# A hybrid layer's compression stage: the sample unit of its mixer spread over two steps, and ScalarE's work around a batch's change in another order

## What is computed

```python
def compress_rows(rows, pe, w1, w2):
    ch = rows[:, :n_chunks * CMP_STRIDE].reshape(B, n_chunks, CMP_STRIDE, G, D)
    proj = jnp.einsum('bnsgd,psdh->pbngh', ch, w1)
    bias = jnp.einsum('psd,psdh->ph', pe, w1)
    h = proj[0, :, 0:n_blk] + bias[0]
    for p in range(1, CMP_PARTS):
        h = h + proj[p, :, p:p + n_blk] + bias[p]
    return jnp.einsum('bngh,hd->bngd', jax.nn.silu(h), w2)
```

```python
def step(s, xs):
    qb, fb, kb, vb = xs
    a = jnp.cumsum(fb.astype(jnp.float32), axis=2)
    decay = jnp.exp(jnp.where(causal, a[:, :, :, None, :] - a[:, :, None, :, :], -jnp.inf))
    att = jnp.einsum('bhtk,bhsk,bhtsk->bhts', qb, kb, decay)
    o = jnp.einsum('bhts,bhsv->bhtv', att, vb) + jnp.einsum('bhtk,bhkv->bhtv', qb * jnp.exp(a), s)
    a_end = a[:, :, -1:, :]
    s = jnp.exp(a_end[:, :, 0, :, None]) * s + jnp.einsum('bhsk,bhsv->bhkv', kb * jnp.exp(a_end - a), vb)
    return s, o
```

## Time and profile before

| | |
|---|---|
| median of 3 runs | 2224.09 us (2223.43 to 2231.28) |
| the profiled execution, device time | 2235.45 us |
| its span, first to last instruction | 2233.7 us |
| TensorE (PE) busy | 2070.1 us, 93% of the span |
| VectorE (DVE) busy | 1455.1 us, 65% |
| ScalarE (ACT) busy | 1088.7 us, 49% |
| GpSimd (POOL) busy | 724.2 us, 32% |
| granted TensorE clock, mean | 0.959 |

### The profile page before, as it was taken

One profiled execution on the slowest core, in us unless ns is written; L12 is line 12 of the kernel. 1 busy time (PEld: TensorE's weight loads), 2 busy tenths in 40 slices (PEclk: granted clock), 3 DMA queues, 4 the chain that ended last, 5 costly groups with the idle time before them and its releaser, 6 DMA issues. The chain is left out here.

```text
span 2233.7 us, 43938 instructions
## 1 busy us (share of the span) xinstructions
PE 2070.1 (93%) x17158; PEld 1931.3 (86%) x17158; DVE 1455.1 (65%) x3124; ACT 1088.7 (49%) x2256; POOL 724.2 (32%) x996
## 2 busy tenths in 40 slices
PE   6999998999999999975889898997999999999997
PEld 5999997988888888864768786877999999999997
DVE  4222234876776776786588687458788788765667
ACT  4114223776776776744377476325333333334334
POOL 0001003766655665520089496120111111110000
PEclk9999998999999999987889799998999999999999
DMA  4115554766656656578310011331332332365342
GB/s 128 57 57 169 195 217 122 215 196 176 188 171 194 192 162 183 157 194 306 103 55 8 5 48 55 107 102 41 101 114 75 101 116 73 101 237 192 117 168 96
DMA packets 226053, 295.71 MB, mean 132 GB/s; under 512 B 23986, under 2 KB 161426, under 8 KB 224658
## 3 DMA queue, kind: packets, MB, share of 16 engines
q1 hardware_dynamic: 199224, 191.65, 28.1%
q0 software_dynamic: 26624, 101.27, 13.9%
HBM read 217.12 MB, written 82.63 MB: 134 GB/s over the span
## 5 line engine op out<-in xcount | busy, mean ns | idle before, releaser
L1568 POOL TENSOR_TENSOR C<-C,a_mt 128x264 f32<-128x264 f32 x66 | 69.2, 1069 | 407.6 <-ACT C L1653 271.9
L3520 PE MATMUL cplain<-a_XH,w1H 128*128 128x256 f32 x512 | 155.7, 304 | 6.4 <-ACT a_hs L3132 6.4
L2087 PE MATMUL f<-a_slot,wd_slot 128*128 128x264 f32 x1176 | 148.2, 285 | 1.6 <-DVE a_slot L1897 0.9
L2050 PE MATMUL f<-a_b,ring 128*128 128x264 f32 x1056 | 143.8, 286 | 4.3 <-DVE a_b L1793 3.7
L2087 PEld LDWEIGHTS f<-a_slot,wd_slot 128*128 128x128 f32 x1176 | 144.8, 188 | 2.5 <-issue 1.6
L3520 PE MATMUL cplain<-a_XL,w1H 128*128 128x256 f32 x512 | 144.9, 283 | 0.0
L3520 PE MATMUL cplain<-a_XH,w1L 128*128 128x256 f32 x512 | 144.6, 283 | 0.0
L3461 PE MATMUL cpt<-ident,X 128*128 128x128 f32 x768 | 119.8, 279 | 22.2 <-DVE a_KTL L3341 8.6
L2050 PEld LDWEIGHTS f<-a_b,ring 128*128 128x128 f32 x1056 | 135.3, 190 | 4.8 <-issue 4.8
L2917 POOL DMA_INDIRECT X<-in_cache_nsa_kv,idx x122 | 129.3, 1060 | 31.3 <-issue 24.2
L502 PE MATMUL pj<-wH,xL 128*128 128x256 f32 (+2 forms) x464 | 130.9, 282 | 0.0
(11 more groups left out here) (623 smaller groups left out, 6551.2 us busy)
## 6 DMA issues: line engine op xcount, KB each, us to landing
v_s<-X SPq DMA_DIRECT2D x64, 256.0 KB, 4.3
a_slot<-a_T SPq DMA_DIRECT2D x20, 792.0 KB, 4.6
raw<-in_w_in POOLq DMA_DIRECT2D x12, 1024.0 KB, 6.1
V<-v_s SPq DMA_DIRECT2D x6, 2048.0 KB, 12.1
raw<-in_w_gate SPq DMA_DIRECT2D x22, 512.0 KB, 5.2
raw_odd<-in_w_val SPq DMA_DIRECT2D x22, 512.0 KB, 6.1
a_T<-C SPq DMA_DIRECT2D x20, 528.0 KB, 3.5
a_T<-sums SPq DMA_DIRECT2D x11, 792.0 KB, 4.5
```

The lines of the kernel that those rows point to most:

```text
L1568: nc.gpsimd.tensor_tensor(C[j][:, at], C[j][:, at], mt[:, q % 2, m, c], ALU.mult).then_inc(multiplied, 1)
L2050: last = nc.tensor.matmul(out_bank(q, r, c), w[:, k], x[:, k], start=begins and k + part == 0, stop=k == 3 and part == 2, skip_group_check ...
L2087: last = nc.tensor.matmul(acc(u, o, h), x(n)[:, k, P * o:P * o + P], a(n)[:, k, HW * h:HW * h + HW], start=u in (0, 2, 4, 6) and begins an ...
L3520: last = nc.tensor.matmul(out[:, h], w, x, start=(begins and q + h + part == 0), stop=(ends and q + h == 2 and part == 2), skip_group_chec ...
```

## The change

Nothing that is computed changes; work changes its place.

- ScalarE: a new piece `load_silu` (one column of Silu into the new tile `tiny`) stands at the end of s=7, so that Silu's table is loaded there. `hidden(u - 1, 0)` moves from the end of s=1 to the end of s=0. The exponentials of the units move from the end of the steps s=3, 5, 7 to the end of s=2, 4, 6; those at s=1 stay. `keys_high` stands ahead of `high_sum`.
- VectorE: `keys` ahead of `low_sum`. For a sample unit, `results` in the odd step behind the first lower part, the first four updates at that step's end as before, and the last four in the next even step, ahead of its weighing.
- TensorE: for a sample unit `decode_products` stand ahead of the second half of `project_second` in the even step; `outputs` behind `project_first` of the odd step; the first half of the new states ahead of the second half of `project_second` there; their second half behind `project_first` of the next even step.

```diff
--- before.py
+++ after.py
@@ -2773,6 +2773,7 @@
         S0 = sb("S0", [P, DB, P])
         ob = sb("ob", [P, 3, P])
         osq = sb("osq", [P, P])
+        tiny = sb("tiny", [P, 1])
         rowsel = sb("rowsel", [DT, DB])
         tokb = sb("tokb", [P, DB, DT])
         normw = sb("normw", [P, HGW])
@@ -2810,7 +2811,7 @@
             "sub_ready", "exp_ready", "w_ready", "a_done", "post_step", "a_kept"))
         b_done, o_kept, s_ready2, sq_ready, sc_step, o_ready, vs_ready = (sem(n) for n in (
             "b_done", "o_kept", "s_ready2", "sq_ready", "sc_step", "o_ready", "vs_ready"))
-        d_done, d_kept = sem("d_done"), sem("d_kept")
+        d_done, d_kept, tiny_ready = sem("d_done"), sem("d_kept"), sem("tiny_ready")
 
         block = ctx.enter_context(nc.Block())
         cache = io["cache_nsa_kv"][0].rearrange("n (c t) s g d -> (n c) (t s g d)", t=2)
@@ -3132,6 +3133,12 @@
                     last = nc.scalar.activation(x, x if k == 0 else plain[m][:], ACT.Silu, bias=bias[:, 2 * k + m:2 * k + m + 1])
                 last.then_inc(hs_ready[k], 1)
 
+            def load_silu(u):
+                act.wait_ge(bias_kept, 1)
+                if u >= 1:
+                    act.wait_ge(tiny_ready, u)
+                nc.scalar.activation(tiny[:], bias[:, 0:1], ACT.Silu).then_inc(tiny_ready, 1)
+
             def hidden_prompt(k):
                 act.wait_ge(rows_turned, k + 1)
                 for m in range(2):
@@ -3218,14 +3225,16 @@
                     copy_turned(at + 1, 1)
                 split_high(at + 1, 1)
                 if at + 1 < PAIRS:
+                    keys_high(at + 1)
                     high_sum(at + 1)
-                    keys_high(at + 1)
-                if u >= 1 and s == 1:
-                    hidden(u - 1, 0)
-                if at % 2 == 1 and at // 2 + 1 < NN:
+                if (s == 1 or s % 2 == 0 and s > 0) and at // 2 + 1 < NN:
                     exponentials(at // 2 + 1)
                 if at % 2 == 0 and at >= 2:
                     squares(at // 2 - 1)
+                if u >= 1 and s == 0:
+                    hidden(u - 1, 0)
+                if s == NS - 1 and u < DB:
+                    load_silu(u)
             for k in range(2):
                 prompt_hidden_rows(k)
             squares(NN - 1)
@@ -3404,13 +3413,17 @@
                 if at + 1 < LAST:
                     upper_copy(at + 1, 0)
                 if at % 2 == 0:
-                    if n >= 1 and not decode(n - 1):
+                    if n >= 1 and decode(n - 1):
+                        decoded(n - 1, 1)
+                    elif n >= 1:
                         results(n - 1)
                     weigh(n)
                 elif not decode(n):
                     pairs(n)
                 if at + 1 < LAST:
                     low_part(at + 1, 0)
+                if at % 2 == 1 and decode(n):
+                    results(n)
                 if u >= 1 and s == 4:
                     keep_blocks(u - 1)
                 if s == NS - 1 and u < DB:
@@ -3419,8 +3432,8 @@
                     upper_copy(at + 1, 1)
                     low_part(at + 1, 1)
                 if at + 1 < PAIRS:
+                    keys(at + 1)
                     low_sum(at + 1)
-                    keys(at + 1)
                 if 1 <= u < DB - 1 and s == 1:
                     queries(u + 1)
                 if at % 2 == 0 and decode(n):
@@ -3429,14 +3442,14 @@
                         block_maxima(0, slice(16, 32))
                         for i in range(2):
                             block_maxima(1, slice(16 * i, 16 * i + 16))
-                    results(n)
                 elif decode(n):
-                    for half in range(2):
-                        if at == LAST - 1:
-                            block_maxima(half, slice(32, 48))
-                        decoded(n, half)
+                    if at == LAST - 1:
+                        for G in range(2):
+                            block_maxima(G, slice(32, 48))
+                    decoded(n, 0)
                 if at == LAST - 3:
                     block_maxima(0, slice(0, 16))
+            decoded(NN - 1, 1)
             for G in range(2):
                 block_maxima(G, slice(48, 64))
             keep_blocks(DB)
@@ -3661,6 +3674,10 @@
                 n = at // 2
                 turn(at + 1, 0)
                 project_first(at)
+                if at % 2 == 1 and decode(n):
+                    outputs(n)
+                elif at % 2 == 0 and n >= 1 and decode(n - 1):
+                    new_states(n - 1, 1)
                 if u >= 1 and s == 4:
                     blocks(u - 1)
                 turn(at + 1, 1)
@@ -3673,6 +3690,10 @@
                 if chunk and n >= 1:
                     wide_products(n)
                     small_products(n, (0, 1))
+                elif at % 2 == 0 and decode(n):
+                    decode_products(n)
+                elif decode(n):
+                    new_states(n, 0)
                 project_second(at, 1, (lambda: score(at)) if late and u < DB else None)
                 if chunk and n >= 1:
                     small_products(n, (2, 3))
@@ -3681,20 +3702,11 @@
                         wide_products(n)
                     small_products(n, (4, 5) if n >= 1 else range(6))
                     turn_keys(n)
-                elif at % 2 == 0:
-                    decode_products(n)
-                elif decode(n):
-                    new_states(n, 0)
-                else:
+                elif at % 2 == 1 and not decode(n):
                     outputs(n)
-                if decode(n):
-                    if at % 2 == 0:
-                        outputs(n)
-                    else:
-                        if at == LAST - 1:
-                            for k in range(2):
-                                turn_prompt(k)
-                        new_states(n, 1)
+            for k in range(2):
+                turn_prompt(k)
+            new_states(NN - 1, 1)
             blocks(DB)
```

## The result

| | before | after |
|---|---|---|
| median | 2224.62 us (4 runs, 2223.43 to 2231.28) | 2204.59 us (4 runs, 2202.58 to 2208.66) |
| ratio after / before, 95% interval | | 0.9906 [0.9882, 0.9931] |
| the profiled execution | 2235.45 us | 2202.58 us |
| its span | 2233.7 us | 2200.8 us |
| cache steps, all 64 | 592.75 us | 572.34 us |

The account below looks back on a forecast made before the run. TensorE was taken to set the pace in the cache steps, with 32 us of waits to win there. The terms sum to 26.6 us, taken off the 2224.09 us median: 2197.5 us forecast, range 2189 to 2212.

Parts of the forecast that it names:

- swap: KTH before SH, KTL before SL: KTL waits in s=7 shorter by 0.34, 2.4 us in all; nothing in s=0.
- sample unit: Cache steps: 3.2 from outputs moved, 3.9 from new states' second half, -3.3 for an added wait, 5.5 from clock falls.
- table load: Silu's load moved from s=0 to the end of s=7: costs nothing, gains 7 x 0.92 = 6.4 us.
- hidden rows, s=2: Moved to the end of s=0, they end TensorE's waits on a_raw and nearly those on a_prow in s=2: 6.2 us.
- exponentials moved: From the end of s=3, 5, 7 to s=2, 4, 6: they fit in ScalarE's idle time and cost nothing.
- hidden rows, prompt: In the prompt's steps the same 1.34 stands ahead of the 3.55 wait for the weighed products: 1.3 us gained.
- last two prompt steps: Fourth sample unit: the wait between the new states' halves is taken apart by other work; 1.0 us, bounds 0 and 1.3.
- new wait: TensorE waits 0.7 for the weighing in the step after a sample unit, KTL 0 to 0.8 late; taken 3 x 1.1.
- So 0.68 stays: In s=0 TensorE arrives 0.92 earlier and still waits 0.68 for KTL, as XL takes 1.36 behind the score copies.
- rival 1: The clock falls as before and the sample unit's added wait is at its upper bound: 17.5 gained, 2206.6 us; chance 0.18.
- rival 3: ScalarE becomes the bound of even steps: 24 x 1.36 = 32.6 us lost against 26.6 gained, 2230.1 us; chance 0.05.
- Rival 2: The pace passes to the gathers of X, only 2.3 us from the prompt's steps counts: 2221.8 us; chance 0.09.

Follow-up runs that it names:

- late_load: The changed kernel with the early Silu table load at the end of s=7 taken out, so it loads in s=0; 2206.72 us, single run.
- squares_first_no_swap: The changed kernel with squares ahead of the exponentials, and SH ahead of KTH, SL ahead of KTL as before the change; 2209.81 us, single run.
- hidden_s1: The changed kernel with the hidden rows put back at the end of s=1, ahead of the Exp load; 2223.64 us, single run.
- act_only: The changed kernel with its sample unit part undone on TensorE and VectorE; ScalarE's and VectorE's other new order stays; 2212.55 us, ratio 0.992.
- exp_odd: The changed kernel with the exponentials back at the end of every odd step; 2198.80 us, ratio 0.9859.
- squares_first: The changed kernel with the squares ahead of the exponentials, these still at the end of even steps; 2198.16 us, ratio 0.9861.

## Why the prediction was right, and where not

The direction, the range (2189 to 2212) and the mechanisms of the gains held: 2204.59 against 2197.5. The cache steps became 20.4 us shorter where 23 to 25 were expected. That the total came this near is in part luck, as errors of the terms cancel: the swap and the sample unit brought 4.5 us more than was put down for them, the table load and the exponentials 6 to 9 us less.

| term | predicted | measured | by |
|---|---|---|---|
| table load | 6.4 | 3.5 to 4.3 | late_load, as measured and 7 x 0.61 |
| swap | 2.4 | 5.1 | squares_first_no_swap |
| hidden rows, s=2 | 6.2 | 6.4 to 8.1 | 6 x (9.99 - 8.93), before to after; hidden_s1 from the second step on |
| sample unit: 3.2 + 3.9 - 3.3 + 5.5 | 9.3 | 11.1 | act_only |
| exponentials moved | 0 | -4.1 to -6.0 | exp_odd, squares_first, against two profiles of the change |
| sum, cache steps | 24.3 | 20.1 to 24.5 | the change itself: 20.4, 22.2 |
| hidden rows, prompt | 1.3 | 1.1 to 1.6 | the wait for a_QA, 3.55 to 2.48; hidden_s1, a single run |
| last two prompt steps | 1.0 | 2.2 | 10.40 + 3.66 to 5.71 + 6.16, from first product to first product, one profile of each |

The terms are not independent: the hidden rows' 8.1 contains the new wait of step 18 (1.48 or 0.57), which is one of the sample unit's.

- **Table load and swap.** The two share s=0: it became 0.95 shorter (10.21 to 9.26) where 0.92 was expected. "So 0.68 stays" held too, as 0.49 on KTL and 0.16 on prow. But the credit was given wrongly. The swap takes 0.34 off s=0 where the prediction gave nothing, and the load only 0.61. Outside s=0 the swap also shortens s=6, which was not foreseen, while in s=7 the KTL wait falls by 0.25 and not by 0.34 (0.43 to 0.18 in most batches, without long copies).
- **Hidden rows.** a_raw is gone from s=2. 0.50 is left on prow where 0.25 was expected. That the transposes and the copies that follow them are the limit sooner than thought is a reading; no run tested it.
- **Sample unit.** The new wait was mis-sized: 3.3 against 1.6 (0.57 in step 18, 0.43 for kvc in step 36, 0.57 in step 54), below its lower bound of 3 x 0.7. The wait itself came a little shorter than the 0.7 worked out, one of the three never came on the weighed products, and no KTL delay was added in these steps; 1.1 had been chosen for it. Against it stands an unforeseen 1.15 on KTL in step 16. It is no new delay of KTL: step 16 takes 9.27, like every other s=0, where the wait is 0.49. With the outputs moved out, TensorE has less to do in that step and reaches KTL earlier, so 0.66 of the 1.52 for attTd was not to be had. That the clock falls go with the waits ahead of them was right: none of the four is in any profile with the new order, and those behind the 1.31 waits and in the first unit's outputs are in both profiles with the old one (before and act_only). So rival 1, that they are no work of the waits, fell.
- **Exponentials: the step that failed.** The prediction said "they fit, and cost nothing". On ScalarE this is true: no odd step waits for raw copies, the sign that rival 3 was to give. But it looked only at the copies of the next step behind them and not at the squares, which stand in between on the same queue. The squares begin 1.25 later (538.54, where the exponentials began at 537.29); that passes through GpSimd and holds VectorE. It costs 4.1 us, and 1.4 more (10.69 against 9.27) in the profile with a clock fall in step 56. Without this one term the kernel would have come out at the 2198 to 2200 us that squares_first gave in its two sets of runs.
- **Rival 2.** The gathers did not take the pace: TensorE waits for no X, at a DMA share of 0.63.
- **The prompt.** 4.4 us against 2.3, but a second profile of the change had 56.39 instead of 57.83 us for these steps, so a difference of 1 us there is not settled by a single profile.

Left open: why GpSimd's train holds VectorE in some units and not in others. Only in the three units behind a sample unit did a train of differences hold a copy. There it did so with starts 0.29, 0.60 and 1.06 behind a_prod (2.61, 2.94 and 3.40 us), and not with 0.11, 0.40 and 1.65, over all the kernels here. In other units the first copy takes 0.29 or less with the train 0.61 or 1.04 to 1.07 behind a_prod, in the changed kernel and, for the latter, before it too. So the shift of the train is shown to be the cause in these units, and why they are open to it is not.

The KTL wait of 1.4 to 1.6 in step 31, before the change too, is a simpler case. In step 31 of after one of the copies takes 1.84 us, and it ends with a single GpSimd operation, by the timeline of GpSimd:

```profile
644.43 1.89 POOL L2900 TENSOR_TENSOR a_vsel<-a_vin,a_rowsel 32x1024 f32<-32x1024 f32 x1
```

This lays out the sampled values for the new states of the sample unit that follows. Where no copy meets it, XL does: 1.19 us in step 31 with the reductions (the KTL wait falls to 0.99) and 2.18 without the swap (1.74). In step 13, an s=5, the same operation holds the first copy for 1.27 us before and 1.78 after, and TensorE does not wait. No run here moved that operation.

## What to carry to other kernels

When a block is moved in an in-order queue, list what now stands behind it, as well as whether the block itself fits; then follow each of these to the next engine. Where two terms act on the same step, price them together and check with the step's length, since each alone depends on what the other has done. A work item that nobody on the critical path waits for can still do harm by when it runs: here a norm's squares set when GpSimd's train ran beside VectorE.

## What the runs showed of the hardware

- A train of GpSimd operations without gaps can hold one VectorE operation for the whole of it: a 32x32 copy took 3.40 us instead of 0.29 (from 540.56 to 543.96; the train is over at 543.93). A reduction beside the same train took 0.50, as always. The Trainium skill, "SBUF — State Buffer", section "Who interferes with whom", says that VectorE shares a pair of ports with GpSimd under an exclusive lock, for copies in some modes and for operations with two SBUF inputs, and not for reductions. The trace agrees with it in what was held, copies and XL and no reduction. The page has the lock last for one instruction. A single GpSimd operation of 1.89 us (a_vsel) fits that, as the copy that it holds ends with it (1.84); beside the train, though, one copy was held over 12 instructions, each 0.28 to 0.39 us, and in other units the same copies got in between them (0.21 to 0.29).
- The clock's fall is not fixed by the wait ahead of it: behind waits of 3.18 and 3.16 us on KTL in the same step of the same kernel it fell to half in one profile (step 56: 10.69 us) and stayed in the other (9.27 us). Of six profiles with a KTL wait of 2.39 to 3.18 us there, five have the fall. The falls behind 1.31 us waits, on the other hand, came in all three units of before and in all three of act_only.
